# State-space end reordered, decay-turning stage dissolved, and the odd output layer begun on HGRN's chunks

## The reference, cut to what matters

```python
proj = jnp.einsum('btd,de->bte', xn, w_in)                       # 4624 columns
q_raw, f_raw, i_raw, g_raw, z, xbc, dt_raw = jnp.split(proj, cuts, axis=-1)
o_c, s_hgrn = gla_chunked(silu(q), k, i, log_f, s_hgrn0, chunk)  # mixer C: HGRN2, 4 heads, 128x128 states
o_c = rms_normalize(o_c).reshape(b, t, vd) * hgrn_gain * jax.nn.silu(g_raw)
xbc_c, conv_new = causal_conv(xbc, conv_buf, conv_w, conv_b)     # conv_new: the last 3 rows, an output
dt = jax.nn.softplus(dt_raw + dt_bias)
a = -jnp.exp(a_log) * dt
y, s_ssm = ssd_chunked(xh * dt[..., None], a, bh, ch, s_ssm0, chunk)   # mixer D: state space, 16 heads x 64
y = y + d_skip[:, None] * xh
y = y.reshape(b, t, D_INNER_D) * jax.nn.silu(z)
y = rms_normalize(y.reshape(b, t, G_D, D_INNER_D // G_D)).reshape(b, t, D_INNER_D) * ssm_gain
out = jnp.einsum('bte,ed->btd', jnp.concatenate([o_c, y], axis=-1), w_out)
```

## Time and profile before

| | us |
|---|---|
| median of 3 timed runs | 1730.38 (1728.35 to 1731.14) |
| profiled execution, its own time | 1720.66 |
| its span, first to last instruction | 1718.8 |
| busy: TensorE / VectorE / ScalarE / GpSimd | 1582.2 / 501.1 / 405.9 / 52.5 |
| mean granted TensorE clock | 0.95 |

### The profile page before, as it was taken

The page is one execution under the profiler, slowest core; times in us unless marked ns, Lnnn a source line. Parts: engine busy times, 40 slices in busy tenths (PEclk is TensorE's granted clock), DMA queues, the critical chain, the costliest instruction groups (busy, mean ns, idle before and its releaser), DMA issues.

```text
span 1718.8 us, 37109 instructions
## 1 busy us (share of the span) xinstructions
PE 1582.2 (92%) x16653; PEld 1197.6 (70%) x16653; DVE 501.1 (29%) x708; ACT 405.9 (24%) x686; POOL 52.5 (3%) x59
## 2 busy tenths in 40 slices
PE   8988799989999966596999999999999999999993
PEld 7976489989899955396346366686766767538562
DVE  5456454443458465643000000100001000000002
ACT  4345343332437466431000000000000000000001
POOL 0000000000000000000000000000000000000000
PEclk9999699998999988696999999999999999999997
DMA  8565435543425425208969999999999999999993
GB/s 323 183 225 174 135 110 167 178 147 123 151 101 196 152 85 123 56 1 354 388 262 385 414 408 411 412 405 417 407 410 411 406 417 406 408 414 409 413 406 152
DMA packets 155288, 478.79 MB, mean 279 GB/s; under 512 B 30152, under 2 KB 57552, under 8 KB 154883
## 3 DMA queue, kind: packets, MB, share of 16 engines
q1 hardware_dynamic: 152028, 467.90, 71.1%
q0 software_dynamic: 2496, 6.84, 1.1%
q10 hardware_dynamic: 615, 1.77, 0.3%
HBM read 463.69 MB, written 12.77 MB: 277 GB/s over the span
## 4 chain that ended last, share of the span: by engine, by line
PE 51%; SPq 2%; issue 1%; DVE 0%; DMA 0%; ACT 0%; POOL 0%; DVEq 0%
PE ps L2672 34%; PE ps L2684 17%; SPq L2344 1%; DMA item_raw<-xn_rows,item_pick 0%; SPq L2337 0%; DVE token_rows L2726 0%; POOL item_raw L2352 0%; DVE token_rows L2737 0%; DVE token_rows L2719 0%; DVEq L2582 0%; ACT act L2767 0%; ACT tail_rows L2767 0%; DVE item_x L2700 0%; ACT row_stat L2774 0%; SPq L2392 0%
## 5 line engine op out<-in xcount | busy, mean ns | idle before, releaser
L2672 PE MATMUL ps<-up_ring,item_x 128*32 128x448 f32 x6144 | 581.9, 540 | 2.9 <-DVE item_x L2700 2.9
L2672 PEld LDWEIGHTS ps<-up_ring,item_x 128*32 128x32 f32 x6144 | 315.8, 110 | 263.9 <-issue 168.7
L2684 PE MATMUL ps<-down_ring,hid_t 128*32 128x256 f32 x5376 | 299.4, 379 | 1.3 <-issue 0.3
L2684 PEld LDWEIGHTS ps<-down_ring,hid_t 128*32 128x32 f32 x5376 | 238.7, 110 | 62.3 <-issue 11.7
L2709 DVE TENSOR_TENSOR hid<-hid,ps 128x1344 f32<-128x1344 f32 x16 | 24.9, 1554 | 718.3 <-PE ps L2672 718.3
L2760 ACT COPY item_y<-ps 128x512 f32<-128x512 f32 x8 | 4.7, 585 | 431.2 <-PE ps L2684 431.2
L1245 PE MATMUL ps<-x_hi_up,w_hi_up 128*128 128x288 f32 x320 | 86.1, 299 | 0.2 <-ACT w_hi_up L490 0.2
L1246 PE MATMUL ps<-x_lo_up,w_hi_up 128*128 128x288 f32 x320 | 86.0, 295 | 0.0
L2758 ACT ACTIVATE hid<-ps 128x1344 f32<-128x1344 f32 x16 | 20.6, 1290 | 239.4 <-PE ps L2672 239.3
L506 PE MATMUL ps<-x_hi_in_odd,w_hi_in_odd 128*128 128x288 f32 x256 | 69.6, 297 | 0.0
L507 PE MATMUL ps<-x_lo_in_odd,w_hi_in_odd 128*128 128x288 f32 x256 | 69.5, 297 | 0.0
(11 more groups left out here) (489 smaller groups left out, 2025.0 us busy)
## 6 DMA issues: line engine op xcount, KB each, us to landing
up_ring<-in_we_dram SPq DMA_DIRECT2D x256, 896.0 KB, 10.3
down_ring<-in_we_dram SPq DMA_DIRECT2D x112, 1024.0 KB, 13.1
ring<-in_w_ffn_dram SPq DMA_DIRECT2D x23, 1024.0 KB, 6.6
ring<-in_w_in_odd_dram SPq DMA_DIRECT2D x9, 2048.0 KB, 7.7
ring<-in_w_in_even_dram SPq DMA_DIRECT2D x6, 2048.0 KB, 9.3
ring<-in_w_ffn_dram SPq DMA_DIRECT2D x5, 2048.0 KB, 7.7
ring<-in_w_out_odd_dram SPq DMA_DIRECT2D x3, 2048.0 KB, 7.9
ring<-in_w_out_even_dram SPq DMA_DIRECT2D x2, 2048.0 KB, 7.8
```

The source lines that it names most:

```text
L2672: mm = pe.matmul(k.ps[32 * q:32 * q + 32, 3 * w + g, 0:FW].rearrange("p (j r) -> p j r", r=GROUP), xg[:, c, g, :], block_of[:, q, :, :], s ...
L2684: mm = pe.matmul(k.ps[32 * q:32 * q + 32, 6 + g // 2, 256 * (g % 2):256 * (g % 2) + 256], hidT[:, 2 * r + j, g, :], block_of[:, j, 256 * q ...
```

## The change

Five things are moved; no product is added or left out but one layout of the last convolution rows.

1. `stage_turn_decays` is gone. Its two writes of `acum` are issued by SyncE at the end of `stage_in_odd`; the reads go to the start of `stage_hgrn` behind the state load; the last convolution rows of prompt and samples are packed together (27 columns, `dta["last"]`, in a part of `proj` that is free by then) by VectorE in group 15 of `stage_in_odd`, and turned by 12 transposes at the end of HGRN. The turned rows lie in `mixed_out[:, 4:12]` until stored; VectorE waits for that store ahead of its first `take` in `stage_ssd`. The decays and the skip weights are turned at HGRN's end too.
2. In `stage_ssd` ScalarE makes decays 6 and 7 ahead of its wait for the prompt state; VectorE scales all eight states at once between score 6 and take 5, and only the additions stay in `new_state`; TensorE does `y_prompt(6)` ahead of the first state products. Some buffers move into `k.act`.
3. ScalarE rounds the four HGRN chunks for the output layer in `stage_ssd` (two `round_pair`), and VectorE takes their rest (two `take_pair`). `source.made = 2` tells the output layer that its first two halves of x are there.
4. The group norm's root and its eight scalings move into the output layer (`GroupNorm`), between its weight splits. From its third half on ScalarE waits there for the state-space stores, for which SyncE no longer waits at the end of `stage_ssd`.
5. The table load is left out in attention, in `stage_ssd` and in the output layer, and follows the first weight rounding in the down projection.

```diff
@@ class SplitInput
+    def round_pair(self, act, n): ...
     def take_pair(self, dve, n):
         at = slice(2 * n, 2 * n + 2)
-        dve.wait_ge(*self.rounded.at(n + 1))
+        dve.wait_ge(*self.rounded.at(n + 1 - self.made))
...
+class GroupNorm:
+    def roots(self, act):
+        act.activation(self.rs, self.rs, ACT.Ln).then_inc(*self.rooted.up())
+        act.wait_ge(*self.rooted.at(1))
+        act.activation(self.rs, self.rs, ACT.Exp, scale=-0.5).then_inc(*self.rooted.up())
+    def scale(self, dve, j):
+        dve.wait_ge(*self.rooted.at(2))
+        y = self.x[:, j, :]
+        dve.scalar_tensor_tensor(y, y, self.k.vec[:, 52 + j:53 + j], self.rs[:, j // 2, :], ALU.mult, ALU.mult).then_inc(*self.scaled.up())
@@ gemm_rows, ScalarE
-                act.preload_act_table_set(LOG_EXP)
                 for h in range(len(halves)):
-                    if source:
+                    if source and h >= source.made:
+                        act.wait_ge(*k.count("stored").all())
+                        act.wait_ge(*norm.scaled.at(2 * (h - source.made) + 2))
                         source.round_pair(act, h)
                     sp_.round_hi(act, h)
+                    if h == 0:
+                        if norm:
+                            norm.roots(act)
+                        else:
+                            act.preload_act_table_set(LOG_EXP)
@@ gemm_rows, VectorE
-                    if source:
+                    if source and h >= source.made:
                         source.take_pair(dve, h)
                     sp_.take_lo(dve, h)
+                    if norm and h < 4:
+                        norm.scale(dve, 2 * h)
+                        norm.scale(dve, 2 * h + 1)
@@ stage_in_odd, VectorE, group 15
+                        dve.wait_ge(*dve_step.all())
+                        dve.tensor_copy(dta["last"][:, :, 0:3], conv_in[:, :, TP:TP + 3]).then_inc(*dve_step.up())
+                        dve.tensor_copy(dta["last"][:, :, 3:27].rearrange("p c (b r) -> p c b r", r=3), conv_in_s[:, :, :, NT:NT + 3])\
+                           .then_inc(*dve_step.up())
@@ stage_hgrn, ScalarE, its end
+                for n in range(3):
+                    act.wait_ge(*last_turned.at(n + 1))
+                    act.copy(last_rows[:, 512 * n:512 * n + 512], k.ps[0:27, 3 + n, :]).then_inc(*last_copied.up())
+                act.wait_ge(*dt_turned.at(1))
...
@@ stage_hgrn, TensorE, its end
+                pe.wait_ge(*n_["mean"].at(3))
+                for n in range(3):
+                    for c in range(4):
+                        mm = pe.transpose(k.ps[0:27, 3 + n, P * c:P * c + P], last[:, 4 * n + c, :], ident)
+                    mm.then_inc(*last_turned.up())
...
@@ stage_ssd, SyncE
-                sp.wait_ge(*n_["stored"].at(80))
@@ stage_ssd, ScalarE
                 decay(5)
+                decay(6)
+                decay(7)
                 act.wait_ge(*n_["state_dot"].at(1))
                 act.copy(statep[:, :, :], k.ps[:, 7, :].rearrange("p (j n) -> p j n", j=8)).then_inc(*n_["statep"].up())
-                decay(6)
+                source.round_pair(act, 0)
+                source.round_pair(act, 1)
```

204 lines of the change are left out of this document (95 added, 109 removed).

## The result

| kernel | median of the timed runs | lowest to highest | profiled execution | its span |
|---|---|---|---|---|
| before | 1727.93 us (6 runs) | 1725.06 to 1731.14 | 1720.66 us | 1718.8 us |
| after | 1700.05 us (6 runs) | 1696.41 to 1704.35 | 1701.23 us | 1699.4 us |

The ratio is 0.9837, with an interval of 0.9818 to 0.9856. That is 28 us off, from 25 to 31; the prediction had 24.1 off and 1706.3 us. The time lies inside the range, 6.3 us under the forecast. Three more runs had moved the median of before from 1730.4 to 1727.9, and that is 2.5 of the 6.3. The other 3.8 are a larger gain.

The account below looks back on a forecast made before the run. Experts were taken as bound by TensorE and full DMA engines, untouched, so time removed ahead of them, where engines wait at stage barriers, comes off one for one. The terms sum to 24.1 off: 1730.4 to 1706.3 us, range 1698 to 1713.

Parts of the forecast that it names:

- The stage that is gone, 10.5: Decay-turning stage before HGRN: its 10.5 us, barrier included, come off, with the moved work priced at nothing.
- HGRN's head, 2.6: HGRN's opening transposes and products run at full clock, so VectorE starts earlier: 2.6 us off, between 0 and 3.1.
- Rival (b): HGRN: half clock in the head loses its 2.6, the tail costs up to 0.8 more; 1709 to 1710, 17%.
- HGRN's tail, -0.4: HGRN's end: added transposes and small products mostly covered by the state's store; cost 0 to 1.2 us, taken as 0.4.
- State-space end, 8.2: State-space stage: reordered decays, no store wait, roots and scalings moved out; 8.2 us off, from 6.5 to 10.
- Output layer's head, 1.9: Odd output layer: only the weights' rounding stands ahead of TensorE, 1.9 us for 3.81; 1.9 us off.
- No wait at the third half: Output layer: the moved VectorE steps are ready before TensorE's third half, not before 734, so no second wait there.
- Rival (c): Output layer: ScalarE's wait for stores holds up later roundings and TensorE starves at the third half; slower, 1735, 2%.
- Table load, 1.3: Down projection: the 1.28 us load moves behind the first rounding, TensorE's wait 4.2 for 5.48; 1.3 us off.
- Rival (a): Group sums and output layer: TensorE keeps its clock, 3 us off and another 2.5; about 1700 to 1702, 27%.
- The sum: Whole kernel: 10.5 + 2.6 - 0.4 + 8.2 + 1.9 + 1.3 = 24.1 us off, to 1706.3.
- gap of 9.7 us between profile and median: Kernel before: profiled execution ran 9.7 us under the median of three timed ones, unexplained and taken as unchanged.

Follow-up runs that it names:

- e5: Changed kernel with the group norm's roots and scalings back at the end of the state-space stage; 1705.29 us, ratio 0.9876 to the kernel before.
- e6: Changed kernel with the state-space end's old order on ScalarE, VectorE and TensorE, roots and scalings staying in the output layer; 1706.02 us, ratio 0.9875.
- e7: Changed kernel with SyncE again waiting for all stores at the end of the state-space stage; 1707.04 us, ratio 0.9895.
- e10: Changed kernel with unread products filling TensorE's stands in the state-space stage and at the head of output layer and down projection; 1699.84 us, ratio 0.9830.
- The parts alone: Kernel before with one part each: decay-turning stage dissolved, 1713.11 us; state-space end reordered, 1712.86; down projection's table load moved and attention's left out, 1723.19.
- e0: The kernel before, unchanged, timed and profiled once more; 1723.63 us, ratio 1.0003.
- e8: Changed kernel with first-half high-part products for all eight output chunks ahead of the low-part wait, in down projection and output layer; 1693.63 us, ratio 0.9796.

## Why the prediction was right, and where not

- **The stage that is gone, 10.5:** 10.5 measured (11.25 to 0.75), in ten profiles out of ten. The packing and the writes in the input layer and the loads at HGRN's head show on no path.
- **HGRN's head, 2.6:** right at the diagonal (3.8 us for 6.4), wrong for the stage. This is the term that was mis-sized. I argued that VectorE starts earlier "since VectorE is what the levels behind it run on". That holds up to the seventh level, where 1.9 us or more of lead are left in every profile; then the output products of TensorE are waited for, and in five profiles of eight they run at the lower clock. In the changed kernel's first profile the 2.6 stayed (HGRN 2.8 shorter), over eight profiles 0.6 are left on average. Rival (b), half clock in the opening products, did not happen, the clock fell behind the diagonal; a price like its 2.6 came at another place in most executions.
- **HGRN's tail, -0.4:** 0 or better. The clock was 1.00 from 650.96 to 655.5, through the transposes and small products that I had put at half rate on one of its bounds, the work ended at 656.6, and the store ended the stage, as argued.
- **State-space end, 8.2:** 9.3. Roots and scalings are worth 5.4 in it, the order 3.9 and the wait for the stores 4.1, each by what its return costs (e5, e6, e7); they overlap. The working held in its structure; VectorE's chain took 12.2 us from its free moment to the last `take` where I had 12.7 to 13.4, and the sums 5.73 where I had 6.6. SyncE's stores came within 0.2 us of the means at the end.
- **Output layer's head, 1.9:** 1.86 (3.81 to 1.95). TensorE's wait was 3.07. No wait at the third half, and all that was moved there is covered (e5). The wait for the stores costs nothing there. Rival (c) was far off: it needed a landing at 728, 10 us into an output layer that I had beginning at 718.0, and the last store landed at 714.6, 3.7 us into one that began at 710.9.
- **Table load, 1.3:** 1.3 by the wait (5.48 to 4.20). The Trainium skill ("ScalarE: Activation LUTs", What ACT_TABLE_LOAD costs) counts 2.66 us for a switch of tables, a drain included. The trace of the kernel before does not agree: its rounding begins 1.30 us after the load does.
- **Rival (a), the clock kept:** it did not happen by itself. Behind the 3.07 us the clock was 1.00 for the first 1.3 us of products and then 0.5:

```profile
712.00:714.00 2.00, 0.79 (x4) 0.56 (x4) 1.16 (x1) 1.97 (x3) 0.00 (x0) 1.00 0.85 217
714.00:716.00 2.00, 0.82 (x3) 0.82 (x4) 2.00 (x3) 2.00 (x2) 0.00 (x0) 0.53 0.07 16
```

  Made to happen (e10), it was worth 2 us in the output layer, not 3, and nothing at the sums, not 2.5, since SyncE's stores end that stage as late as the sums do. The measured 1700.05 lies on this rival's 1700 to 1702, and that is chance: its mechanism was not there.
- **The sum:** 10.5 + 0.6 + 9.3 + 1.9 + 1.3 = 23.6 us by stages on average over the profiles (25.8 in the first one), 27.9 (25 to 31) by the first timing and 27 (22 to 32) by the second. The parts alone gave 11.6, 11.9 and 1.6 by their medians. Whether the 2 to 4 us over the stages are there at all, or are the spread of executions, these runs don't settle. That my 24.1 is so near the stages' 23.6 is in part luck: 2.0 us too much for the head stand against 0.4 and 1.1 too little for the tail and the state-space end. I had left the gap of 9.7 us between profile and median unexplained and taken it as unchanged. It was not: the changed kernel's profile lay 1.2 us over its median. Its likely part is what e0 showed: up to the input layer's end the granted clock was 0.96 in the first profile of before and 0.94 in e0.

## What to carry to other kernels

This stage, which was only there to turn and to copy, was worth its whole length once its work lay beside another stage's, and that sum could be made from the timeline to a tenth. A gain that rests on the clock could not: here it was mostly given back in a later part of the same stage, in five profiles of eight. So price such a gain low, and where a stand can be filled, try real work first: e8's high products gave the best ratio, and dead products held up a barrier and a first real product (both in e10). Where several engines end a stage within a few microseconds of each other, as VectorE and the landing of the stores did here, taking out one of them alone pays only up to the next. Before a profile of before is taken as the base, compare the granted clock of its stages with a second one: eight of the microseconds between two profiles here belonged to neither kernel.
